# Inverse norms of q and k moved from ScalarE and VectorE to GpSimd, with a k|v projection in two parts, in a two-layer hybrid transformer kernel

## The chip, the cores and the metric

The kernel runs on one core of one Trainium2 chip. The metric is the device time of one execution in microseconds. All numbers are float32; TensorE gets its operands as pairs of a high and a low half (`_hi` and `_lo`), and a product is three matmuls, hi by hi, hi by lo and lo by hi.

## What is computed

Two layers work on 512 image tokens `x` and 256 context tokens `ctx`, 1024 wide. The change touches the part that makes q, k and v for the attention of 4 heads:

```python
q = (rmsnorm(q_lat, qc_g) @ w_q_up).reshape(b, n, MLA_HEADS, QK_DIM)
kv = (rmsnorm(kv_lat, kvc_g) @ w_kv_up).reshape(b, n, MLA_HEADS, NOPE_DIM + V_DIM)
q_nope = rmsnorm(q[..., :NOPE_DIM], qn_g)
q_rope = rmsnorm(q[..., NOPE_DIM:], qr_g)
k_nope = rmsnorm(kv[..., :NOPE_DIM], kn_g)
v = kv[..., NOPE_DIM:]
k_rope = rmsnorm(k_rope, kr_g)
if rope is not None:
    q_rope = apply_axial_rope(q_rope, cos[:, None, :], sin[:, None, :])
    k_rope = apply_axial_rope(k_rope, cos, sin)
```

`rmsnorm(x, g)` is `x * rsqrt(mean(x*x) + 1e-6) * g`. NOPE_DIM and V_DIM are 128, the rope part is 64 wide. Around it stand the adaptive norms, the other inputs of the mixer (pooling, gated convolution), softmax, the output projection and a feed-forward block with a convolution. In the second layer only x goes on, so q is made for 4 tiles of 128 tokens there, and for 6 in the first; k and v are made for 6 in both.

## The kernel before

Each engine has its own program, and the order in it is written out by hand; semaphores with counted values tie them together. PSUM is four slots of two banks (2 x 512 columns), used in turn. A `Job` is one use of a slot: `open` waits until its use before is read out, `filled` and `ready` say that TensorE has written it, `last_read` and `taken` that it is read out.

The stage of this change comes after the latents are projected, normed and transposed. For each tile t of 128 tokens:

- TensorE: `project_q(t)` (L808), `project_kv(t)` (L819: 3 matmuls of 512 columns for k, 3 for v, into the two banks of one slot), then `turn(t-1)` (L830), four transposes of q and four of k, and `turn_rope(t-2)` (L843).
- ScalarE, `stats(t)` (L1240): the square of q (L1248), a copy of q into `qn` (L1252), the square of k into `kn` (L1255), the roots of the mean squares (`root_part`, L1237) for the rope part of q, the plain part of q, and k, with the copy `v_hi` (L1259) before the last. Then `turned_hi(t-1)` (L1270), q and k, and `rope_out(t-2)` (L1278).
- VectorE, `normed(t)` (L1730): the sums over heads (L1720), the reciprocals of the roots (L1727), the scaling of q's rope part (L1744), the scaling of k (L1749, out of PSUM), and `v_lo` (L1753, through L1568), whose end frees the slot. Then `turned_lo(t-1)` (L1569).
- GpSimd: it first turns k_rope for all tiles (`rotate`, L559 to L565), then for each q tile it scales the plain part of q (L624), turns the rope part (L634, L636, L640), and makes its high half (L643) and low half (L645) in `q_rs`.

`b_rot` counts 5 steps a tile: L634, L636, L640, high, low. Between tile 1 and tile 2, k_rope is transposed (`krT`), copied out by ScalarE in two copies (L1327, L1328) and halved by VectorE. After the tiles come the scores: the first part of the first score needs tiles 0 to 3, the second part the k of tiles 4 and 5, that is, tile 5's turned slot read out. The table for Exp is loaded by an activation on `warm` (L1334) before the last `turned_hi`.

## Time and profile before

| | us |
|---|---|
| median of 3 runs | 1451.29 |
| lowest and highest | 1451.26, 1451.75 |
| the profiled execution | 1451.35 |
| its span | 1449.6 |

The profile comes from one execution. Its span is measured from the first to the last instruction, so 1.75 us of the execution's own time lie outside it. Times in a row count from the start of the span. In rows of instructions in order of time, the first number is the start, the second the time taken (of all together where `x2` or more stand there), then engine, line, operation, what it writes and reads with its shape, and in brackets how long the engine stood idle just before and who ended that. PE is TensorE, PEld its weight loads, DVE VectorE, ACT ScalarE, POOL GpSimd.

### The profile page before, as it was taken

The numbers are of one execution on the slowest core, as the hardware profiler recorded it, in microseconds if no ns is written. First come the engines' busy times: TensorE is split into PE (matmuls) and PEld (weight loads), VectorE is DVE, ScalarE is ACT, GpSimd is POOL, SyncE is SP. The second block draws the span as 40 slices with busy tenths as digits, with TensorE's granted clock in tenths as the row PEclk, the third lists the DMA queues.
The fourth block names the chain that finished last, engine by engine and source line by source line (L and its number), as shares of the span: only waits on it lengthen the run. The fifth ranks groups of instructions, "written<-read, shape, count | busy, mean of one in ns | idle before, by whom it ended". The sixth has DMA issues, their size and how long they took to land.

```text
span 1449.6 us, 20646 instructions
## 1 busy us (share of the span) xinstructions
PE 1416.5 (98%) x7940; PEld 1224.0 (84%) x7940; DVE 996.3 (69%) x1532; ACT 521.2 (36%) x841; POOL 86.7 (6%) x125
## 2 busy tenths in 40 slices
PE   6999899999999999999999999989999999999998
PEld 3788798889888888888888888878999888888887
DVE  5587887779866666666575678788667555555555
ACT  4352865243231122122221225476445323223322
POOL 0023700000000000000000000350000000000000
PEclk9999999999999999999999999999999999999999
DMA  9742012423543333324333412301032223322324
GB/s 389 296 131 88 1 45 73 146 88 119 184 146 117 94 122 117 121 81 158 116 100 102 144 45 64 111 15 56 4 103 91 98 90 100 99 87 89 112 91 142
DMA packets 42968, 158.62 MB, mean 109 GB/s; under 512 B 5152, under 2 KB 6560, under 8 KB 41760
## 3 DMA queue, kind: packets, MB, share of 16 engines
q1 hardware_dynamic: 42912, 157.87, 32.7%
q8 instruction: 36, 0.59, 0.2%
q14 instruction: 20, 0.16, 0.0%
HBM read 155.76 MB, written 2.10 MB: 109 GB/s over the span
## 4 chain that ended last, share of the span: by engine, by line
PE 84%; DVE 9%; ACT 3%; DMA 2%; issue 2%; SPq 0%; DVEq 0%; ACTq 0%
PE ps L734 68%; PE ps L653 4%; PE ps L655 4%; PE ps L654 4%; DVE w_lo L1428 1%; DMA ada_step<-in_w_step 1%; DVE tmp L1553 1%; DVE H_lo L1562 1%; PE ps L882 1%; PE ps L667 1%; DVE ss L1495 1%; DVE nmax L1771 1%; DMA w_raw<-in_w_main 1%; DVE pt_lo L1568 1%; ACT w_hi L1072 1%
## 5 line engine op out<-in xcount | busy, mean ns | idle before, releaser
L734 PE MATMUL ps<-H_hi,w_hi 128*128 128x512 f32 (+1 forms) x1280 | 448.8, 351 | 3.9 <-DVE H_lo L1562 2.6
L734 PE MATMUL ps<-H_lo,w_hi 128*128 128x512 f32 (+1 forms) x1280 | 447.4, 350 | 0.0
L734 PE MATMUL ps<-H_hi,w_lo 128*128 128x512 f32 (+1 forms) x1280 | 447.1, 349 | 0.0
L1072 ACT ACTIVATE w_hi<-w_raw 128x1024 fp32r<-128x1024 f32 x180 | 187.5, 1055 | 421.8 <-PE ps L734 368.8
L734 PEld LDWEIGHTS ps<-H_hi,w_hi 128*128 128x128 f32 x1280 | 242.3, 189 | 37.4 <-DVE H_lo L1562 3.8
L734 PEld LDWEIGHTS ps<-H_hi,w_lo 128*128 128x128 f32 x1280 | 242.2, 189 | 31.6
L734 PEld LDWEIGHTS ps<-H_lo,w_hi 128*128 128x128 f32 x1280 | 242.3, 189 | 30.8
L1575 DVE SCALAR_TENSOR_TENSOR X<-ps,mod,X 128x512 f32<-128x512 f32 (+1 forms) x296 | 181.1, 645 | 110.4 <-PE ps L734 88.1
L1428 DVE TENSOR_TENSOR w_lo<-w_raw,w_hi 128x1024 fp32r<-128x1024 f32 x180 | 221.7, 1242 | 37.3 <-ACT w_hi L1072 36.3
L734 PE MATMUL ps<-inner_hi,w_hi 128*128 128x512 f32 (+1 forms) x528 | 188.1, 356 | 0.3 <-DVE X L1575 0.3
L734 PE MATMUL ps<-inner_lo,w_hi 128*128 128x512 f32 (+1 forms) x528 | 187.5, 355 | 0.0
L734 PE MATMUL ps<-inner_hi,w_lo 128*128 128x512 f32 (+1 forms) x528 | 187.0, 354 | 0.0
L1926 DVE SCALAR_TENSOR_TENSOR tmp<-ps,vec,tmp 128x511 f32<-128x511 f32 (+1 forms) x132 | 87.3, 661 | 132.6 <-ACT tmp L1399 124.9
L1439 DVE SCALAR_TENSOR_TENSOR ada_out<-ada_raw,cb 128x1024 f32<-128x1024 f32 x107 | 130.7, 1222 | 5.5 <-DVE mod L1445 0.8
L734 PEld LDWEIGHTS ps<-inner_hi,w_hi 128*128 128x128 f32 x528 | 100.3, 190 | 15.0 <-DVE X L1575 0.5
L734 PEld LDWEIGHTS ps<-inner_lo,w_hi 128*128 128x128 f32 x528 | 100.2, 190 | 13.8
L734 PEld LDWEIGHTS ps<-inner_hi,w_lo 128*128 128x128 f32 x528 | 100.0, 189 | 14.1
L1399 ACT ACTIVATE tmp<-ps,vec 128x768 f32<-128x768 f32 (+1 forms) x44 | 35.0, 795 | 198.5 <-PE ps L734 198.5
L1942 DVE TENSOR_TENSOR ff_v<-tmp,ps 128x768 f32<-128x768 f32 (+1 forms) x44 | 36.1, 820 | 74.7 <-PE ps L734 74.4
L1402 ACT ACTIVATE tmp<-tmp 128x768 f32<-128x768 f32 (+1 forms) x44 | 32.6, 740 | 71.3 <-DVE tmp L1926 71.3
L1125 ACT ACTIVATE H_hi<-tmp,mod 128x256 fp32r<-128x256 f32 (+1 forms) x67 | 38.4, 574 | 39.8 <-DVE tmp L1553 39.8
L1079 ACT ACTIVATE tmp<-X 128x256 f32<-128x256 f32 (+1 forms) x61 | 29.4, 487 | 63.7 <-DVE X L1575 54.9
(210 smaller groups left out, 1836.7 us busy)
## 6 DMA issues: line engine op xcount, KB each, us to landing
w_raw<-in_w_main SPq DMA_DIRECT2D x182, 512.0 KB, 3.3
ada_raw<-in_w_ada SPq DMA_DIRECT2D x73, 512.0 KB, 4.1
ada_step<-in_w_step SPq DMA_DIRECT2D x7, 2048.0 KB, 16.7
X<-in_x SPq DMA_DIRECT2D x2, 1024.0 KB, 6.5
cb<-in_cvec SPq DMA_DIRECT2D x2, 1024.0 KB, 7.2
out_x<-X SPq DMA_DIRECT2D x8, 256.0 KB, 4.0
rtab<-in_rope SPq DMA_DIRECT2D x4, 384.0 KB, 9.2
X<-in_ctx SPq DMA_DIRECT2D x1, 1024.0 KB, 19.5
```

The source lines that it names most:

```text
L653: pe.matmul(out, wh[wsl], xh[xsl], start=first, stop=False)
L654: pe.matmul(out, wh[wsl], xl[xsl], start=False, stop=False)
L655: return pe.matmul(out, wl[wsl], xh[xsl], start=False, stop=last)
L734: ins = pe.matmul(job.ps(a, b), ww[:, wsl], xx[:, xk, a:b], start=first and n == 0, stop=last and n == 2)
L1072: act.activation(w_hi[c % 4][:], w_raw[c % 2][:], ACT.Copy).then_inc(chunk_hi, 1)
L1125: act.activation(H[0][:, kk, a:b], tmp[kk % 2][:, a:b], ACT.Identity, bias=mod[L][:, sg, m:m + 1]).then_inc(h_hi[nn], 1)
L1399: act.activation(tmp[par][:, 0:w], g.ps(0, w), ACT.Copy, scale=tap).then_inc(ff_mid[L], 1)
L1428: dve.tensor_tensor(w_lo[c % 4][:], w_raw[c % 2][:], w_hi[c % 4][:].bitcast(F32), ALU.subtract).then_inc(chunk_lo, 1)
L1439: dve.scalar_tensor_tensor(ada_out[:], ada_raw[n % 2][:], 1.0, cb[n >= ADA_A2][:, s], ALU.mult, ALU.mult, accum_out=mod[L][:, s, bass.ds(c ...
L1575: last = dve.scalar_tensor_tensor(xo, job.ps(a - o, b - o), mod[L][:, s, bass.ds(gate + m, 1)], xo, ALU.mult, ALU.add)
L1926: ins = dve.scalar_tensor_tensor(y, g.ps(a + s0, b - 1 + s0), vec[:, bass.ds(L * V_LAYER + V_FC + FT * tap + t, 1)], y, ALU.mult, ALU.add)
L1942: u.last_read(dve.tensor_tensor(ff_v[:, 0:w], tmp[par][:, 0:w], u.ps(0, w), ALU.mult))
```

## The change

**Power instead of root and reciprocal.** ScalarE's `root_part` and VectorE's `inverse` are gone. VectorE adds EPS times the width to the sums (`with_eps`), and GpSimd raises the result to the power -0.5 (`inverse_root_q`, 8 columns, and `inverse_root_k`, 4 columns), reading a tile of -0.5. The missing square root of the width goes into the gains (`rtab`, `qg`). VectorE waits for `b_rc` of GpSimd before it scales q and k.

**Place of the powers.** Those of tile 0 stand within `rotate`, those of tile t+1 behind the addition that ends the turn of tile t. The high half of the turned q becomes a ScalarE copy, `rotated_hi(t-1)`, in `stats(t)` between the square of k and `v_hi`.

**k|v.** Where the slot is the one of the tile before, the three k matmuls wait only for the scaling of that tile's k (`k_nm`) and raise `k_full` for ScalarE's square; the three v matmuls wait for the slot as before.

**Last tile, table.** For tile 5 k is halved ahead of q; its `v_lo` comes after `turned_lo(4)`. The Exp table is loaded right behind the latents' root.

```diff
@@ GpSimd
-        def rotate(src, n, tab, done, before, scratch):
+        def rotate(src, n, tab, done, before, scratch, root_q, root_k):
             pool.tensor_tensor(a, src, rtab[:, tab, 0:n], ALU.mult).then_inc(done, 1)
+            root_q(0)
             for h in range(2):
...
             last.then_inc(done, 1)
+            root_k(0)
             pool.wait_ge(done, before + 2)
...
+            def inverse_root_q(t):
+                pool.wait_ge(b_rt[L], parts(L, t, "q"))
+                pool.tensor_tensor(part_rms[:, t % 2, 0:8], part_sums[:, t % 2, 0:8], part_pow[:, 0:8], ALU.pow).then_inc(b_rc[L], 1)
+
+            def inverse_root_k(t):
+                pool.wait_ge(b_rt[L], parts(L, t, "k"))
+                pool.tensor_tensor(part_rms[:, t % 2, 8:12], part_sums[:, t % 2, 8:12], part_pow[:, 8:12], ALU.pow).then_inc(b_rc[L], 1)
...
                 pool.tensor_tensor(src, rgain[:], rope_b[:], ALU.add).then_inc(b_rot[L], 1)
-                pool.wait_ge(b_rot[L], 5 * t + 3)
+                if t + 1 < qtok(L):
+                    inverse_root_q(t + 1)
+                if t + 1 < TOK:
+                    inverse_root_k(t + 1)
+                pool.wait_ge(b_rot[L], 5 * t + 4)
                 hi, lo = (q_rs[L][t % 2][:, :, ROPE * n:ROPE * (n + 1)] for n in range(2))
-                pool.tensor_copy(hi.bitcast(F32R), src).then_inc(b_rot[L], 1)
-                pool.wait_ge(b_rot[L], 5 * t + 4)
                 pool.tensor_tensor(lo, src, hi, ALU.subtract).then_inc(b_rot[L], 1)
@@ TensorE, project_kv
-                job.open(pe)
+                follows = t and JOB[("kv", t), L] - JOB[("kv", t - 1), L] == 4
+                if follows:
+                    pe.wait_ge(k_nm[L], t)
+                else:
+                    job.open(pe)
+                mm3(job.ps(0, 512), kvl, (slice(None), tsl), slot(c0 + C_HD + 2), (slice(None), slice(0, 512)),
+                    True, True).then_inc(k_full[L], 1)
+                if follows:
+                    job.open(pe)
@@ ScalarE
             act.activation(lat_ss[:], lat_ss[:], ACT.Sqrt).then_inc(lat_rt[L], 1)
+            act.activation(warm[:, 0:1], ones[:, 0:1], ACT.Exp)
...
+            def rotated_hi(t):
+
+                act.wait_ge(b_rot[L], 5 * t + 3)
+                src = qn[t % 2][:, 0:ROPES].rearrange("p (h f) -> p h f", h=HEADS)
+                act.activation(q_rs[L][t % 2][:, :, 0:ROPE].bitcast(F32R), src, ACT.Copy).then_inc(b_rot[L], 1)
...
+                act.wait_ge(k_full[L], t + 1)
+                act.activation(kn[t % 2][:], job.ps(0, 512), ACT.Square).then_inc(b_sq[L], 1)
+                if 0 < t <= qtok(L):
+                    rotated_hi(t - 1)
                 job.ready(act)
...
-                root_part(t, "k")
@@ VectorE
+            def with_eps(t, first, last):
+
+                cols = slice(4 * KINDS.index(first), 4 * KINDS.index(last) + 4)
+                dve.wait_ge(b_sum[L], sections(L, t, last))
+                dve.tensor_tensor(part_sums[:, t % 2, cols], part_sums[:, t % 2, cols], part_eps[:, cols],
+                                  ALU.add).then_inc(b_rt[L], 1)
...
                 if t < qtok(L):
-                    inverse(t, "rope", "nope")
+                    dve.wait_ge(b_rc[L], parts(L, t, "q"))
...
+                if t < TOK - 1:
+                    value_lo(t)
...
+            value_lo(TOK - 1)
             turned_lo(TOK - 1)
```

GpSimd in layer 0, from k_rope's turn into tile 1, before:

```order
29 L559 TENSOR_TENSOR win_p<-latr,rtab 128x384
30 L561 TENSOR_TENSOR win_r<-latr,rtab 128x6x32 x2
31 L565 TENSOR_TENSOR latr<-win_p,win_r 128x6x64
32 L624 TENSOR_TENSOR qn_128<-qn_128,part_rms 128x512
33 L634 TENSOR_TENSOR rgain<-qn_128,rtab 128x256
34 L636 TENSOR_TENSOR rope_b<-qn_128,rtab 128x4x32 x2
35 L640 TENSOR_TENSOR qn_128<-rgain,rope_b 128x256
36 L643 CAST q_rs_124<-qn_128 128x4x64
37 L645 TENSOR_TENSOR q_rs_124<-qn_128,q_rs_124 128x4x64
38 L624 TENSOR_TENSOR qn_129<-qn_129,part_rms 128x512
```

The same place in the changed kernel:

```order
32 L566 TENSOR_TENSOR win_p<-latr,rtab 128x384
33 L630 TENSOR_TENSOR part_rms<-part_sums,part_pow 128x8
34 L569 TENSOR_TENSOR win_r<-latr,rtab 128x6x32 x2
35 L634 TENSOR_TENSOR part_rms<-part_sums,part_pow 128x4
36 L574 TENSOR_TENSOR latr<-win_p,win_r 128x6x64
37 L642 TENSOR_TENSOR qn_130<-qn_130,part_rms 128x512
38 L652 TENSOR_TENSOR rgain<-qn_130,rtab 128x256
39 L654 TENSOR_TENSOR rope_b<-qn_130,rtab 128x4x32 x2
40 L658 TENSOR_TENSOR qn_130<-rgain,rope_b 128x256
41 L630 TENSOR_TENSOR part_rms<-part_sums,part_pow 128x8
42 L634 TENSOR_TENSOR part_rms<-part_sums,part_pow 128x4
43 L665 TENSOR_TENSOR q_rs_126<-qn_130,q_rs_126 128x4x64
```

The powers of tile 0 (rows 33 and 35) stand inside k_rope's turn, those of tile 1 (41 and 42) behind the addition that ends tile 0's turn (L658, once L640), and the cast is gone.

ScalarE in layer 0, tile 2 and what follows it, before:

```order
103 L1248 ACTIVATE q_sq_122<-ps 128x768
104 L1252 ACTIVATE qn_128<-ps 128x768
105 L1255 ACTIVATE kn_130<-ps 128x512
106 L1237 ACTIVATE part_rms<-part_sums,vec 128x4 x2
107 L1259 ACTIVATE v_hi<-ps 128x4x128
108 L1237 ACTIVATE part_rms<-part_sums,vec 128x4
109 L1270 ACTIVATE q_hi<-ps,qg 128x4x128
```

In the changed kernel:

```order
102 L1273 ACTIVATE q_sq_124<-ps 128x768
103 L1277 ACTIVATE qn_130<-ps 128x768
104 L1280 ACTIVATE kn_132<-ps 128x512
105 L1263 ACTIVATE q_rs_127<-qn_131 128x4x64
106 L1284 ACTIVATE v_hi<-ps 128x4x128
107 L1298 ACTIVATE q_hi<-ps,qg 128x4x128
```

Three roots are gone, and the copy of tile 1's turned q (row 105) stands between the square of tile 2's k and the copy of its v; in tile 1 the copy of tile 0's q stands in the same place.

## Rows read from the trace of the kernel before

**Rows 1.** The page, busy us, share of the span and instructions, TensorE and others.
```profile
PE 1416.5 (98%) x7940; PEld 1224.0 (84%) x7940; DVE 996.3 (69%) x1532; ACT 521.2 (36%) x841; POOL 86.7 (6%) x125
```

**Rows 2.** Busy time of each engine by stretch, the two stretches of the head projections.
```profile
core 0: us, PE busy (x) PEld busy (x) DVE busy (x) ACT busy (x) POOL busy (x), PEclk, DMA share, GB/s
...
140.00:182.00 42.00, 38.28 (x222) 30.94 (x222) 35.66 (x75) 35.45 (x74) 30.85 (x47) 1.00 0.00 1
...
950.00:984.00 34.00, 29.23 (x160) 23.02 (x160) 28.70 (x56) 26.21 (x53) 18.39 (x29) 0.95 0.00 1
```

**Rows 3.** Waits of TensorE's weight loads, 138 to 182: total, times, longest.
```profile
PEld ps L653 <- DVE v_lo L1568: 2.7, 4, 1.0
PEld ps L837 <- issue: 2.4, 2, 2.1
```

**Rows 4.** The same, 952 to 988.
```profile
PEld ps L653 <- DVE v_lo L1568: 2.2, 2, 1.3
```

**Rows 5.** In order of time, GpSimd, layer 0, k_rope's turn and tile 0.
```profile
142.48 1.16 POOL L561 TENSOR_TENSOR win_r<-latr,rtab 128x192 f32<-128x192 f32 x2
...
143.72 1.16 POOL L565 TENSOR_TENSOR latr<-win_p,win_r 128x384 f32<-128x384 f32 x1
...
144.84 1.03 POOL L624 TENSOR_TENSOR qn<-qn,part_rms 128x512 f32<-128x512 f32 x1
...
147.48 0.80 POOL L640 TENSOR_TENSOR qn<-rgain,rope_b 128x256 f32<-128x256 f32 x1
```

**Rows 6.** In order of time, ScalarE, tile 1 and the square of tile 2's q.
```profile
145.56 0.60 ACT L1255 ACTIVATE kn<-ps 128x512 f32<-128x512 f32 x1
...
147.23 0.79 ACT L1327 ACTIVATE kr_hi<-ps 64x768 fp32r<-64x768 f32 x1
...
150.03 0.81 ACT L1248 ACTIVATE q_sq<-ps 128x768 f32<-128x768 f32 x1
```

**Rows 7.** In order of time, VectorE, scaling in tile 1 and 4, first sums.
```profile
147.07 0.62 DVE L1744 TENSOR_TENSOR qn<-qn,part_rms 128x256 f32<-128x256 f32 x1
...
147.81 0.69 DVE L1749 TENSOR_TENSOR kn<-ps,part_rms 128x512 f32<-128x512 f32 x1
...
151.20 1.00 DVE L1720 TENSOR_REDUCE part_sums<-q_sq 128x4 f32<-128x256 f32 x2
...
156.03 1.00 DVE L1720 TENSOR_REDUCE part_sums<-q_sq 128x4 f32<-128x256 f32 x2
...
163.13 0.88 DVE L1744 TENSOR_TENSOR qn<-qn,part_rms 128x256 f32<-128x256 f32 x1
...
166.66 1.00 DVE L1720 TENSOR_REDUCE part_sums<-q_sq 128x4 f32<-128x256 f32 x2
```

**Rows 8.** Instructions of one line: count, duration in ns least/median/most, first and last start.
```profile
L1237 ACT ACTIVATE part_rms<-part_sums,vec x32: 283/297/325, 142.6 to 972.9; 128x4 f32<-128x4 f32 x32
...
L1727 DVE RECIPROCAL part_rms<-part_rms x22: 164/178/196, 143.3 to 973.3; 128x4 f32<-128x4 f32 x12, 128x8 f32<-128x8 f32 x10
...
L607 POOL TENSOR_TENSOR win_r<-win_r,vec x12: 199/202/1181, 96.4 to 935.4; 128x8 f32<-128x8 f32 x12
...
L1445 DVE TENSOR_TENSOR mod<-mod,vec x8: 155/160/208, 138.1 to 852.3; 128x7 f32<-128x7 f32 x2, 128x5 f32<-128x5 f32 x2, 128x8 f32<-128x8 f32 x2, 128x16 f32<-128x16 f32 x1
```

**Rows 9.** In order of time, the end of the stage in layer 0, TensorE and ScalarE.
```profile
170.34 0.63 PE L837 MATMUL ps<-ident,qn 128*128 128x128 f32 x4 [1.88 <-POOL qn L624]
...
170.49 1.28 ACT L1334 ACT_TABLE_LOAD   x1
...
174.06 0.39 PE L653 MATMUL ps<-k_hi,q_hi 128*128 128x256 f32 x1 [0.66 <-DVE k_lo L1569]
```

**Rows 10.** In order of time, layer 1, GpSimd's turn of tile 0 and tile 1's scaling.
```profile
953.63 0.74 POOL L640 TENSOR_TENSOR qn<-rgain,rope_b 128x256 f32<-128x256 f32 x1
...
953.97 0.68 DVE L1744 TENSOR_TENSOR qn<-qn,part_rms 128x256 f32<-128x256 f32 x1
```

**Rows 11.** Busy time by stretch, with the granted clock, near the end in layer 1.
```profile
974.00:976.00 2.00, 1.67 (x6) 1.54 (x7) 1.44 (x3) 1.97 (x4) 0.00 (x0) 0.57 0.01 4
```

More of the change, by code:

```diff
@@ L359, in halves @@
         nq = qtok(L)
+        if t == TOK - 1 and t < nq:
+            return 2 * t + {"k": 1, "q": 2}[kind]
         return 2 * t + {"q": 1, "k": 2}[kind] if t < nq else nq + t + 1
@@ L548, in _ @@
         pool.memset(lat_ss[:], 1.0).then_inc(consts, 1)
+        pool.memset(part_eps[:, 0:4], ROPE * EPS)
+        pool.memset(part_eps[:, 4:12], NOPE * EPS)
+        pool.memset(part_pow[:], -0.5)
         pool.memset(part_sums[:], 1.0).then_inc(consts, 1)
@@ L640, in _ @@
                 pool.tensor_tensor(src, rgain[:], rope_b[:], ALU.add).then_inc(b_rot[L], 1)
-                pool.wait_ge(b_rot[L], 5 * t + 3)
+                if t + 1 < qtok(L):
[3 more added lines that the diff above has]
+                pool.wait_ge(b_rot[L], 5 * t + 4)
                 hi, lo = (q_rs[L][t % 2][:, :, ROPE * n:ROPE * (n + 1)] for n in range(2))
-                pool.tensor_copy(hi.bitcast(F32R), src).then_inc(b_rot[L], 1)
-                pool.wait_ge(b_rot[L], 5 * t + 4)
                 pool.tensor_tensor(lo, src, hi, ALU.subtract).then_inc(b_rot[L], 1)
+            for t in range(qtok(L) + 1, TOK):
+                inverse_root_k(t)
     @block.tensor
@@ L822, in project_kv @@
                 job = Job(JOB[("kv", t), L])
-                job.open(pe)
-                for half in range(2):
-                    cols = slice(512 * half, 512 * (half + 1))
-                    last = mm3(job.ps(512 * half, 512 * (half + 1)), kvl, (slice(None), tsl), slot(c0 + C_HD + 2),
-                               (slice(None), cols), True, True)
-                job.filled(last)
+                follows = t and JOB[("kv", t), L] - JOB[("kv", t - 1), L] == 4
[7 more added lines that the diff above has]
+                    job.open(pe)
+                job.filled(mm3(job.ps(512, 1024), kvl, (slice(None), tsl), slot(c0 + C_HD + 2), (slice(None), slice(512, 1024)),
+                               True, True))
             def turn(t):
@@ L1267, in turned_hi @@
                 job.ready(act)
-                for kind, dst, o, scale in (("q", q, 0, qg[:, 0:1]), ("k", k, 512, V(L, V_KN))):
+                for kind, dst, o, scale in turned_parts(t):
                     if kind == "k" or t < qtok(L):
@@ L1333, in _ @@
                 rope_out(t - 2)
-            act.activation(warm[:, 0:1], ones[:, 0:1], ACT.Exp)
             turned_hi(TOK - 1)
+            if qtok(L) == TOK:
+                rotated_hi(TOK - 1)
             for t in range(TOK - 2, TOK):
@@ L1721, in sums @@
                                   ALU.add).then_inc(b_sum[L], 1)
-            def inverse(t, first, last):
-                x = part_rms[:, t % 2, 4 * KINDS.index(first):4 * KINDS.index(last) + 4]
-                dve.wait_ge(b_rt[L], sections(L, t, last))
-                dve.reciprocal(x, x).then_inc(b_rc[L], 1)
-                dve.wait_ge(b_rc[L], parts(L, t, "k" if last == "k" else "q"))
+            def with_eps(t, first, last):
[3 more added lines that the diff above has]
+                                  ALU.add).then_inc(b_rt[L], 1)
             def normed(t):
@@ L1736, in normed @@
                     sums(t, "nope", q_sq[L][:, ROPES:HEADS * HQ], NOPE)
+                    with_eps(t, "rope", "nope")
                 dve.wait_ge(b_sq[L], parts(L, t, "k"))
                 sums(t, "k", kn[m][:], NOPE)
+                with_eps(t, "k", "k")
                 if t < qtok(L):
-                    inverse(t, "rope", "nope")
+                    dve.wait_ge(b_rc[L], parts(L, t, "q"))
                     Job(JOB[("q", t), L]).taken(dve)
@@ L1753, in normed, with turned_parts @@
                 job.last_read(lo_half(v[1][:, :, tsl], job.ps(512, 1024).rearrange("p (h f) -> p h f", h=HEADS), v[0][:, :, tsl]))
+            def turned_parts(t):
+                order = (("q", q, 0, qg[:, 0:1]), ("k", k, 512, qg[:, 1:2]))
+                return order[::-1] if t == TOK - 1 else order
             def turned_lo(t):
@@ L1758, in turned_lo @@
                 job = Job(JOB[("turn", t), L])
-                for kind, dst, o, scale in (("q", q, 0, qg[:, 0:1]), ("k", k, 512, V(L, V_KN))):
+                for kind, dst, o, scale in turned_parts(t):
                     if kind == "k" or t < qtok(L):
```

31 lines of the change are left out of this document (14 added, 17 removed).

## The prediction

> **What bounds the kernel now.** The first thing to read is the busy share of the page: TensorE is busy 98% of the span [rows 1]. Whatever lengthens or shortens the waits of TensorE therefore moves the end almost one for one, and anything on another engine counts only through such a wait. The table of stretches then shows where there is anything to win or lose: the stretch of the head projections, 140 to 182 us in layer 0 and 950 to 984 us in layer 1, is the one in which the others are nearly as full as TensorE: in layer 0 VectorE 35.7, ScalarE 35.5 and GpSimd 30.9 of 42 us, and in it TensorE has holes [rows 2]. The waits of TensorE's weight loads in that stretch name the holes: 2.7 us in 4 waits for v_lo, which frees the accumulator of the k|v projection, and 2.4 us, nearly all of it one wait, for the last tile's normed q [rows 3]; in layer 1 the v_lo wait in front of a projection is 2.2 us in two waits [rows 4]. So at most some 5 us a layer are there to be won, and the change aims at about half of them.
>
> All four engines run the tiles in a fixed order, one tile of 128 tokens about every 5 us. GpSimd is the one that is late at the start: its turning of k_rope (L559, L561, L565) ends at 144.84, and only then comes q of tile 0; it leaves the rotation of tile 0 (L640, from 147.48, 0.80 long) at 148.28 [rows 5]. At that time VectorE has long scaled q and k of tile 1, at 147.07 and 147.81 [rows 7], and ScalarE is already copying k_rope out, from 147.23 [rows 6]. In the kernel before nobody but the rope transposes and the next copy of q waits for this lateness.
>
> **Roots off ScalarE, power on GpSimd.** ScalarE loses 32 roots of 0.297 us and VectorE 22 reciprocals of 0.178 us; VectorE gains 22 additions of EPS, of the form of L1445, 0.160 us, each of which has to wait for the reduction before it (0.03 us past its end), so VectorE's work for a tile stays at 4.8 to 4.9 us against 4.83 now (151.20 to 156.03) [rows 7, 8]. GpSimd gains 22 powers. No row shows a power. The nearest is a multiplication of the same shape, 128x8: 199 ns at the least, 202 in the median, and 1181 where it lies beside a long VectorE addition [rows 8]. I take 0.30 us for 8 columns and 0.25 for 4, near the low end since the shape is the same and only the arithmetic is dearer, and keep 0 and 1.18 us as ends.
>
> The Trainium skill (GPSIMD Engine Reference, 3.1 Elementwise) says that branching on data costs about 12 cycles an element at 1.2 GHz; an estimate by it for 8 elements a lane is 0.08 us on top of the row's 0.20, so 0.28 us, and the sum would be 0.1 us a layer lower. No run here shows it yet.
>
> **Where the powers stand is what costs.** The order of GpSimd's instructions puts the powers of tile t+1 behind the rotation of tile t. Step by step for layer 0: the power of q of tile 0 waits for the sums and the added EPS on VectorE, and starts near 142.8, where the next piece of the k_rope turn used to start at 142.48: 0.3 us. It takes 0.3, the power of k 0.25. So the k_rope turn ends 0.8 us later, near 145.65, and the rotation of tile 0, which is 3.4 us behind that [rows 5], at 149.05. Only then can the power of tile 1 run. VectorE gets it at 149.4 instead of having its own reciprocal by 147.07: q of tile 1 is scaled 2.3 us late, k of tile 1 (149.75 against 147.81) 1.9 us late [rows 7]. TensorE's k half of tile 2 now waits for exactly that k, so its earlier start by one v_lo (0.6 us) is spent there.
>
> **The copy that moved to ScalarE.** The high half of the turned q (a GpSimd cast) is now a ScalarE copy of about 0.36 us, placed between the square of k and the copy of v of the next tile. ScalarE runs in order: in tile 1 it ends the square of k at 146.05 (145.56 and 0.49 to the next) and then stands until GpSimd has turned tile 0, at 149.1. Queued behind it are v of tile 1, both copies of k_rope, q and k of tile 0 and the square of q of tile 2. Before, 1.67 us lay between the square of k and the k_rope copy (147.23 less 145.56) [rows 6]; now 0.49, a wait of 3.1, 0.36 and 0.48, so 4.4: the k_rope copy and all behind it come 2.7 us later, the square of q of tile 2 near 152.75 instead of 150.03. VectorE's first sum of tile 2 comes at 153.85 instead of 151.20 [rows 7], 2.65 us late, and the transposes of tile 1 wait on TensorE for k_rope's bank.
>
> **What is won back.** From tile 2 on GpSimd needs 4.15 us and two powers, 4.7, a tile, VectorE 4.88, ScalarE less. Before, VectorE's starts of tiles 2 and 5 are 15.46 us apart (151.20 to 166.66), 5.15 a tile: it waited for TensorE's k|v in each, and one scaling of q was stretched to 0.88 us [rows 7]. Three tiles at 4.88 are 14.64, so 0.8 us comes back; if the stretch, 0.45 us, returns, 0.35. This is the gain of the k half with its own waits: real, and about a third of the loss. Layer 0 at tile 5: 1.85 to 2.3 us late.
>
> **The tail.** The table load of Exp (1.28 us) stands before the last q and k copies; TensorE's last turn starts at 170.34 and its k transposes would release them near 171.4, so removing the load is worth 0.5 us, not 1.28 [rows 9]. It moves behind the root of the latents, 50 us ahead of the stage, where ScalarE has idle time and TensorE does not wait: nothing. The k copies ahead of q gain nothing by themselves, since the second part of the first score waits until both are done and the bank is released by the last. Against this the last scaling of q on GpSimd now stands behind the power of k and the low half of tile 4, which used to be through before: 0.7 us. So the tail is 0.15 to 0.3 us longer. v's rest moved behind the split of the tile before costs nothing in layer 0; in layer 1 its bank is the one that the first score needs, which now starts up to 0.7 us later.
>
> **The sum.** I carried these durations through both orders, row by row; for the kernel before this gives tile 5's k within 0.6 us of the trace. Layer 0 comes out 2.8 us later at the first row maximum; with the stretch of 0.45 us counted as gone, and the load's place in doubt, I take 2.5. Layer 1 has the same order and the same place: its rotation of tile 0 runs from 953.63 to 954.37 while tile 1's q is scaled at 953.97 [rows 10]; it has only four q tiles, so two k-only tiles are left in which k waits for the power. It comes out 3.0 later. There the clock falls too: TensorE is granted 0.57 of full speed on average in 974 to 976 [rows 11], so part of it is at 1.2 GHz, after three waits of TensorE; with longer waits there the low stretch may grow by the 0.3 us I add. Sum 2.5 and 3.3 = 5.8 us. The profiled execution took 1451.35 us with a span of 1449.6; the median is 1451.29, the same within 0.06. Forecast 1457.1 us. A difference under 0.2% (2.9 us) can't be told from none here.
>
> **The rivals.** (a) *The late start is made up for*: TensorE's holes close so far that the tiles run at its own 4.8 us, and the fall of the clock in layer 1 is gone. For it: the v_lo waits are real, 2.7 and 2.2 us [rows 3, 4]. Against it: GpSimd sets the start, and 0.35 us a tile is all there is. It gives 1452.8: 2.65 late, less 4 tiles by 0.35 and 0.5 of table in each layer, is 0.75 each. Chance 0.17. (b) *Faster*: the powers cost nothing, and the waits of VectorE and ScalarE on GpSimd in tile 1 are absorbed before TensorE needs k and q of tile 2. Then the gain is what v_lo costs now, up to 0.6 us in six places, and the table: 1451.3 less 4 is 1447.3. It decides if the rotation of tile 0 ends before about 147.0, where tile 1's scaling stood; it ends at 148.28 already now [rows 5]. Chance 0.08. (c) *A dear power*: at 0.8 and 0.5 us GpSimd's tile is 5.45 us and it becomes the bound of every tile: 5.1 and 4.7 late, 1461.1; at 1.18 and 0.8 some 17 us, 1468. The point is 0.7 us for both powers, where GpSimd passes VectorE's 4.88. For it: the 1181 ns; against: that figure comes beside one VectorE addition. Chance 0.13. (d) The forecast, 0.62, with its own range of 1454.3 to 1459.5 (powers free and the stretch gone, 1.2 and 1.8 late; powers of 0.5 and 0.4, 3.8 and 3.8, with clock).
>
> GpSimd and VectorE share their path into SBUF, says the Trainium skill (GPSIMD Engine Reference, 1. Specifications), for VectorE instructions with two SBUF inputs; the rows that were stretched, 882 against 426 ns, are of that kind. By it the added EPS and the powers could stretch each other by tenths of a microsecond, which lies within the range.
>
> **How the numbers follow.** Low end 1452.5: (b) and the part of (a) below it are left out, about 0.12. High end 1462.5: the dearer half of (c) is left out, 0.07. Slower by over 0.2%: (d) and (c), 0.75; within 0.2%: (a), 0.17; faster: (b), 0.08.
>
> **What would show it.** The GpSimd power row near 0.3 us; ScalarE waiting about 3 us for GpSimd's rotation in front of the q_rs copy of tile 1, in each layer, and about 1 us at later tiles; VectorE waiting 1.5 us and more for the power before the scaling of tile 1's q, and nearly nothing later; first sum of tile 2 at 153.5 to 154; tiles 2 to 5 at 4.9 us apart; v_lo gone from TensorE's waits in front of projections, k (kn) and k_rope's bank there instead; first row maximum 2.5 us later in layer 0 than at 175.55. I am wrong if ScalarE's wait in tile 1 is under 1 us, if a power is over 0.7 us, or if the later tiles run under 4.7 us apart.

## The result and the profile after

The changed kernel takes 1476.68 us (median; 1474.76 to 1477.10), the kernel before on the same chip 1451.51 (1451.26 to 1451.75). The ratio is 1.0171 with a 95% interval of 1.0159 to 1.0184: 25 us slower. The forecast was 1457.1 with a range up to 1462.5, so the sign was right and the size was not.

The page, busy time of each engine, after (against [rows 1]):

```profile
PE 1423.0 (97%) x7940; PEld 1228.7 (83%) x7940; DVE 995.2 (68%) x1534; ACT 519.3 (35%) x819; POOL 108.7 (7%) x140
```

GpSimd has 22 us more work, from 86.7 to 108.7, and the kernel became 25 us longer. An engine that is busy for 7% of the span does not look like a bound; in the stretch of the head projections it is one. By stretch, with the columns of [rows 2], after (the stage is 13 us longer in layer 0 now, so the window is wider):

```profile
138.00:192.00 54.00, 42.29 (x217) 34.00 (x217) 36.24 (x71) 30.85 (x55) 43.49 (x53) 0.91 0.00 1
178.00:180.00 2.00, 0.00 (x0) 0.00 (x0) 0.69 (x3) 2.00 (x4) 2.00 (x2) 1.00 0.00 0
180.00:182.00 2.00, 0.00 (x0) 0.00 (x0) 1.76 (x3) 0.06 (x1) 2.00 (x4) 0.92 0.00 0
182.00:184.00 2.00, 1.96 (x10) 1.99 (x11) 0.84 (x2) 0.00 (x0) 1.92 (x4) 0.50 0.00 0
```

GpSimd, 43.5 of 54 us, is now the fullest engine, ahead of TensorE. From 178 to 182 us TensorE does nothing at all, and right behind it its granted clock is 0.50, 1.2 GHz. It falls to 0.50 in 148 to 150 and 162 to 164 us too, each time behind four microseconds in which TensorE was busy for 1.45 and 2.21 us. Before, layer 0 had 1.00 over the whole stretch [rows 2].

One line's instructions on GpSimd, after, the two powers: count, duration in ns least/median/most.

```profile
L630 POOL TENSOR_TENSOR part_rms<-part_sums,part_pow x10: 1647/1650/1662, 141.8 to 984.4; 128x8 f32<-128x8 f32 x10
...
L634 POOL TENSOR_TENSOR part_rms<-part_sums,part_pow x12: 1007/1012/1015, 144.7 to 995.5; 128x4 f32<-128x4 f32 x12
```

These two rows are the main finding. The prediction had 0.30 and 0.25 us. The multiplication of the same shape, 202 ns [rows 8], was no guide, and 1.18 us, which the prediction kept as the upper end, was too low as well. The spread over ten is 15 ns: this is a price, not a disturbance.

In order of time, after, GpSimd from the end of tile 0's rotation to tile 1's scaling, and the scalings of the next tiles (against [rows 5]):

```profile
149.28 0.73 POOL L658 TENSOR_TENSOR qn<-rgain,rope_b 128x256 f32<-128x256 f32 x1
149.96 1.65 POOL L630 TENSOR_TENSOR part_rms<-part_sums,part_pow 128x8 f32<-128x8 f32 x1
151.58 1.01 POOL L634 TENSOR_TENSOR part_rms<-part_sums,part_pow 128x4 f32<-128x4 f32 x1
152.56 0.73 POOL L665 TENSOR_TENSOR q_rs<-qn,q_rs 128x256 f32<-128x256 f32 x1
153.24 1.04 POOL L642 TENSOR_TENSOR qn<-qn,part_rms 128x512 f32<-128x512 f32 x1
...
160.56 1.04 POOL L642 TENSOR_TENSOR qn<-qn,part_rms 128x512 f32<-128x512 f32 x1
...
167.33 1.04 POOL L642 TENSOR_TENSOR qn<-qn,part_rms 128x512 f32<-128x512 f32 x1
```

From 160 to 170 us no row of GpSimd has a wait ahead of it: it runs from one instruction into the next, and its tile is 6.77 us (160.56 to 167.33). The prediction's 4.15 us without powers and 1.65 + 1.01 make 6.81. Before it was 5.15 a tile, and VectorE's and TensorE's work set it.

The same seen from VectorE, in order of time, after (against [rows 7]):

```profile
151.65 0.43 DVE L1776 TENSOR_TENSOR qn<-qn,part_rms 128x256 f32<-128x256 f32 x1 [2.43 <-POOL part_rms L630]
...
156.01 0.99 DVE L1750 TENSOR_REDUCE part_sums<-q_sq 128x4 f32<-128x256 f32 x2
...
162.47 1.00 DVE L1750 TENSOR_REDUCE part_sums<-q_sq 128x4 f32<-128x256 f32 x2
...
169.22 1.00 DVE L1750 TENSOR_REDUCE part_sums<-q_sq 128x4 f32<-128x256 f32 x2
```

And as a list of waits, 138 to 192 us, after (total, times, longest; against [rows 3]):

```profile
ACT q_rs L1263 <- POOL qn L658: 10.4, 5, 4.9
DVE qn L1776 <- POOL part_rms L630: 7.2, 6, 2.4
PEld ps L675 <- DVE kn L1780: 5.7, 4, 2.2
PEld ps L864 <- issue: 5.3, 3, 4.6
```

The largest waits of ScalarE and VectorE behind the stage's first square end at GpSimd. TensorE's waits for k (kn) in front of the k half are those that the own waits of the halves were to shorten; in layer 0 v_lo is no longer the one that is waited for there, k is.

A yardstick for the rest is **the length of the stage**: from ScalarE's first square of q to VectorE's first row maximum. It leaves out how early or late the stage begins. In layer 0 it was 34.84 us (140.71 to 175.55) and is 48.06 (139.65 to 187.71); in layer 1 it was 30.95 and is 41.84. Together 24.1 us, which is the whole loss within about 1 us; nothing outside the stage needs an explanation. Layer 0's 13.2 us split into 5.9 up to the first sum of tile 2, 4.5 in the three tiles from there to tile 5, and 2.8 in the tail.

### The profile page after: what moved, and what is told of

Same layout as the page of the kernel before. It is cut to its first block, busy times and chain, and to the rows that moved or that the text cites. A ratio compares the mean times of both kernels' runs of the same rounds, so it can differ in the third digit from the quotient of the medians.

```text
span 1472.9 us, 20629 instructions
## 1 busy us (share of the span) xinstructions
PE 1423.0 (97%) x7940; PEld 1228.7 (83%) x7940; DVE 995.2 (68%) x1534; ACT 519.3 (35%) x819; POOL 108.7 (7%) x140
## 4 chain that ended last, share of the span: by engine, by line
PE 83%; DVE 8%; POOL 3%; ACT 2%; DMA 2%; issue 2%; SPq 0%; POOLq 0%; DVEq 0%; ACTq 0%
PE ps L756 68%; PE ps L675 4%; PE ps L676 3%; PE ps L677 3%; DVE w_lo L1457 1%; POOL part_rms L630 1%; DMA ada_step<-in_w_step 1%; PE ps L909 1%; DVE ss L1524 1%; POOL part_rms L634 1%; PE ps L689 1%; DMA w_raw<-in_w_main 1%; DVE nmax L1812 1%; DVE tmp L1582 1%; DVE pt_lo L1597 1%
```

## The experiments

The theory: the mechanism of rival (c), *a dear power*, with the powers in GpSimd's own queue in each tile, costs some 18 us, and what the forecast described (late rotation, ScalarE's wait for it) costs the rest. The rival theory: the order and its waits cost nearly all of it. The expectations call a "hand-worked sequence" what the prediction used too: the durations of the rows carried through each engine's order, row by row, here with the measured price of the power. Each ratio is taken against the kernel before run beside it, whose median lay between 1450.5 and 1451.5 us.

### The price taken away

```diff
-  pool.tensor_tensor(part_rms[:, t % 2, 0:8], part_sums[:, t % 2, 0:8], part_pow[:, 0:8], ALU.pow).then_inc(b_rc[L], 1)
+  pool.tensor_tensor(part_rms[:, t % 2, 0:8], part_sums[:, t % 2, 0:8], part_pow[:, 0:8], ALU.mult).then_inc(b_rc[L], 1)
```

The same is done for the 4 columns of k.

> The changed kernel with a multiplication in place of each of the 22 powers, on the same engine, tiles and waits. It leaves out the inverse norms of q's and k's parts (their sums are multiplied by -0.5 instead), so the rest is computed at another scale. Theory, the price: the power measures 1.65 us for 128x8 and 1.01 us for 128x4 where the prediction had 0.30 and 0.25, and this alone makes GpSimd the bound of every tile (tiles 6.8 us apart). Working the sequence of one tile through with 0.2 us for each, the shift of the first row maximum against the kernel before falls from 12.9 to 2.5 us in layer 0 and from 10.8 to 2.7 in layer 1, so 1451.5 + 5.2 = 1456.7 us, tiles 4.8 to 5.0 us apart. Rival, the place: the powers stand in GpSimd's order behind the rotation and in front of q's scaling, and the halves and the moved copy add their own waits; most of the 25 us is then left, 1470 us or more, whatever the operation costs.

Measured: 1457.71 us, ratio 1.0048 (1.0033 to 1.0064), some 7 us over the kernel before. The stage is 2.7 us longer in layer 0 and 3.7 in layer 1. The operation alone is worth 18 us (1.0171 less 1.0048, of 1451; by the medians 19); the place and the waits are worth the 7 that remain. This run is the experiment of the forecast: a power of 0.20 us where it had assumed 0.30 and 0.25, and 1457.7 us where it had forecast 1457.1. Against the kernel before run beside it (1450.5) that is 7.0 us, where 5.8 was forecast. In order of time, this kernel, ScalarE and VectorE in tile 1, then VectorE's first sums:

```profile
148.24 0.42 ACT L1263 ACTIVATE q_rs<-qn 128x256 fp32r<-128x256 f32 x1 [2.76 <-POOL qn L658]
...
148.41 0.43 DVE L1776 TENSOR_TENSOR qn<-qn,part_rms 128x256 f32<-128x256 f32 x1 [0.99 <-POOL part_rms L630]
148.75 0.68 DVE L1780 TENSOR_TENSOR kn<-ps,part_rms 128x512 f32<-128x512 f32 x1
...
152.89 0.99 DVE L1750 TENSOR_REDUCE part_sums<-q_sq 128x4 f32<-128x256 f32 x2
...
157.84 1.00 DVE L1750 TENSOR_REDUCE part_sums<-q_sq 128x4 f32<-128x256 f32 x2
...
163.07 1.01 DVE L1750 TENSOR_REDUCE part_sums<-q_sq 128x4 f32<-128x256 f32 x2
...
168.31 1.01 DVE L1750 TENSOR_REDUCE part_sums<-q_sq 128x4 f32<-128x256 f32 x2
```

The stage begins 0.68 us earlier here (140.03) than in the kernel before. ScalarE waits 2.8 us for the rotation, and the first sum of tile 2 is 2.4 us late. But the next tiles are 4.95, 5.23 and 5.24 us apart, not 4.88. From 157.84 to 168.31 VectorE has no wait on record:

```profile
157.84:168.31 10.47, 10.00 (x60) 8.23 (x60) 10.15 (x21) 8.50 (x16) 8.93 (x17) 1.00 0.01 2
```

VectorE, 10.15 of 10.47 us, is full (third of the busy times, as in [rows 2]). In order of time, the same kernel, the EPS additions of tile 2 and tile 3, then one pass between VectorE and GpSimd:

```profile
153.92 0.17 DVE L1757 TENSOR_TENSOR part_sums<-part_sums,part_eps 128x8 f32<-128x8 f32 x1
...
158.88 0.45 DVE L1757 TENSOR_TENSOR part_sums<-part_sums,part_eps 128x8 f32<-128x8 f32 x1
...
159.95 0.16 DVE L1757 TENSOR_TENSOR part_sums<-part_sums,part_eps 128x4 f32<-128x4 f32 x1
160.19 0.33 POOL L634 TENSOR_TENSOR part_rms<-part_sums,part_pow 128x4 f32<-128x4 f32 x1 [0.59 <-DVE part_sums L1757]
...
163.81 0.73 POOL L658 TENSOR_TENSOR qn<-rgain,rope_b 128x256 f32<-128x256 f32 x1
...
164.12 0.45 DVE L1757 TENSOR_TENSOR part_sums<-part_sums,part_eps 128x8 f32<-128x8 f32 x1
...
165.19 0.17 DVE L1757 TENSOR_TENSOR part_sums<-part_sums,part_eps 128x4 f32<-128x4 f32 x1
```

VectorE's addition of EPS to the 8 sums of q takes 0.17 us in tile 2, where GpSimd does nothing beside it, and 0.45 in the later tiles, where it lies beside GpSimd's last step of the rotation (L658) and ends with it. That is the difference between 4.95 and 5.24 us. It repeats: the addition for k (159.95) lets GpSimd's instruction for k go, GpSimd works through scaling and rotation without a wait until 164.5, the stretched addition ends there, and the next addition for k comes at 165.19, 5.24 us after the one before. From tile 2 on VectorE's scaling of k also starts just as GpSimd's instruction for k ends, a wait too short to be listed. ScalarE's copy is not in this loop: the square of q that is queued behind it ends near 162.5, and VectorE takes it up at 163.07, straight behind its work for the tile before. This is read from the rows; no run takes the stretch away alone. The expectation of the run with the copy back on GpSimd, below, still puts the loop through ScalarE's wait.

### How the time answers to the price

The same with one of the two powers left in, and with q's power run a second time for each tile but the first (`part_two` is read by nobody):

```diff
                     inverse_root_q(t + 1)
+                    pool.tensor_tensor(part_two[:], part_sums[:, t % 2, 0:8], part_pow[:, 0:8], ALU.pow)
```

> The changed kernel with the multiplication in place of q's power (128x8) alone; k's power (128x4, 1.01 us) stays. It leaves out the inverse norms of q's parts. Theory: beyond what is hidden, each added us of GpSimd's work comes out in every tile. By the hand-worked sequence 12.6 us over the kernel before where it has 5.2 for two multiplications and 23.6 for two powers: 1451.3 + 12.6 = 1463.9 us, a little over that since the measured times of the others were 0.9 to 1.8 above it. Rival, a step: once the powers together pass some length an order of waits tips over and nearly the whole loss is there; then this run is at 1472 or more, or, if the length isn't reached, at 1458.

> The changed kernel with the multiplication in place of k's power (128x4) alone; q's power (128x8, 1.65 us) stays. It leaves out the inverse norms of k's parts. By the hand-worked sequence 15.0 us over the kernel before: 1451.3 + 15.0 = 1466.3 us or a little more. Rival: k's power, which stands behind q's and ahead of the low half and of q's scaling, is the one that stalls the tile; then this run is near that with multiplications alone, 1458 us.

> The changed kernel with q's power of each tile but the first run a second time, into a tile that nobody reads: five more powers of 1.65 us on GpSimd in each layer, a tile where q's are computed (three in layer 1). If GpSimd's own sequence sets the tiles, as the 6.8 us between tiles say, each comes out in full: 1.65 us x 8 = 13.2 us over the changed kernel, 1476.7 + 13 = 1490 us. Rival: the tile is set by waits for VectorE or ScalarE, and GpSimd has slack; then the added powers are hidden in part, under 1485 us.

| kernel | power of q and k of a tile, us | median, us | ratio (95%) | stage longer, layer 0 and 1 |
|---|---|---|---|---|
| multiplications | 0.20 and 0.26 | 1457.71 | 1.0048 (1.0033 to 1.0064) | 2.7, 3.7 |
| k's power alone | 0.21 and 1.08 | 1465.66 | 1.0100 (1.0083 to 1.0116) | 7.6, 7.1 |
| q's power alone | 1.65 and 0.20 | 1468.18 | 1.0118 (1.0101 to 1.0135) | 9.1, 7.4 |
| the changed kernel | 1.65 and 1.01 | 1476.68 | 1.0171 (1.0159 to 1.0184) | 13.2, 10.9 |
| q's power twice | 3.29 and 1.01 | 1488.88 | 1.0258 (1.0241 to 1.0275) | 21.9, 15.9 |

Expected were 1456.7, 1463.9 "or a little over", 1466.3 "or a little more", and 1490: all four within about 2 us. The three runs with a multiplication in them leave out the inverse norms that it stands for. There is no step. Between the changed kernel and the doubled power 12.2 us come for 8 added instructions of 1.65 us, 13.2: nearly every one in full. Between the multiplications and the changed kernel 10 x 1.45 and 12 x 0.75 us are added, 23.5 us, and 18 to 19 arrive: the first tenths of each tile go into GpSimd's slack. The doubled power's tiles, in order of time, VectorE:

```profile
167.58 1.01 DVE L1752 TENSOR_REDUCE part_sums<-q_sq 128x4 f32<-128x256 f32 x2
...
175.92 1.00 DVE L1752 TENSOR_REDUCE part_sums<-q_sq 128x4 f32<-128x256 f32 x2
...
184.27 1.00 DVE L1752 TENSOR_REDUCE part_sums<-q_sq 128x4 f32<-128x256 f32 x2
```

8.34 us apart, where the changed kernel has 6.77: 1.57 more for one more power.

### The price by itself

```diff
+        for n, x in enumerate((2.0, -0.5)):
+            pool.memset(probe[n][:], x).then_inc(b_ms[0], 1)
+        for m, (op, other) in enumerate(((ALU.pow, 1), (ALU.pow, 0), (ALU.mult, 1))):
+            for n in (1, 2, 4, 8, 16, 32):
...
+                pool.tensor_tensor(probe[2][:, 0:n], probe[0][:, 0:n], probe[other][:, 0:n], op).then_inc(b_ms[0], 1)
```

> The kernel before with 18 added instructions at the start of GpSimd's program, one behind the other, on tiles that nothing else uses: the power of 128 x 1, 2, 4, 8, 16 and 32 values 2.0 to the exponent -0.5, the same with exponent 2.0, and the multiplication of the same tiles. Only their rows count, not the time. Theory: the power is paid by the element, about 0.16 us a column on a start of 0.37 us (1.65 us for 8 columns and 1.01 for 4 in the changed kernel give this line), so 0.53 us for 1 column, 0.69 for 2, 2.9 for 16, 5.5 for 32, the same for both exponents; the multiplication stays near 0.20 us. Rival: most of the cost is a fixed start that comes with every power, or it depends on the exponent; then 16 and 32 columns stay well under those numbers, or the two exponents differ.

Groups of instructions by shape, GpSimd (xcount, then busy us and mean ns of one). The first two rows are from the stretch of the powers to -0.5, the third is a power to 2.0, the last two are from the stretch of the multiplications:

```profile
L559 POOL TENSOR_TENSOR probe<-probe,probe 128x32 f32<-128x32 f32 x1 | 5.4, 5427 | 0.1
...
L559 POOL TENSOR_TENSOR probe<-probe,probe 128x1 f32<-128x1 f32 x1 | 0.6, 561 | 0.1
...
L559 POOL TENSOR_TENSOR probe<-probe 128x32 f32<-128x32 f32 x1 | 5.4, 5445 | 0.1
...
L559 POOL TENSOR_TENSOR probe<-probe,probe 128x32 f32<-128x32 f32 x1 | 0.3, 312 | 0.1
...
L559 POOL TENSOR_TENSOR probe<-probe,probe 128x8 f32<-128x8 f32 x1 | 0.2, 207 | 0.1
```

For the exponent -0.5 the six widths took 561, 711, 1007, 1637, 2900 and 5427 ns: 157 ns a column of 128 (4866 ns over 31 columns) on 0.40 us. The exponent 2.0 costs the same (561 to 5445). The line was drawn beforehand from 8 and 4 columns alone and gave 0.53, 0.69, 2.9 and 5.5. The multiplications took 191 to 608 ns with no order in their width (312 for 32 columns, 608 for 2), so a price a column can't be read from them; the three from 542 to 608 ran beside two long VectorE instructions (L1560 and L1569 of that kernel). With 312 ns for 32 columns it is far under the power's 5427. The power's cost is paid by the column, and by this line joining q's and k's powers in one instruction would save no more than the 0.40 us (an estimate; it was not run).

### The copy alone, and the copy undone

```diff
@@ ScalarE, kernel before with the copy moved (undone the other way round)
                     root_part(t, "nope")
+                if 0 < t <= qtok(L):
+                    rotated_hi(t - 1)
                 act.activation(v[0] ...
@@ GpSimd
-                pool.tensor_copy(hi.bitcast(F32R), src).then_inc(b_rot[L], 1)
```

> The kernel before with one edit: the copy of the rotated q's high half moves from GpSimd to ScalarE, at the place where the change has it (behind the square root's step of the next tile, ahead of v's eviction); square root and reciprocal stay. By the hand-worked sequence ScalarE waits about 3 us for GpSimd's rotation in the second tile, and the first row maximum comes 3.3 us later in layer 0 and 2.8 in layer 1: 1451.5 + 6.1 = 1457.6 us. Rival: the copy is free, since ScalarE has slack and GpSimd gains 0.5 us a tile: 1451.5 or under.

> The changed kernel with one part undone: the copy of the rotated q's high half is back on GpSimd. That takes ScalarE's waits for the rotation away (10.4 us in five tiles of layer 0) and puts 0.47 us a tile on GpSimd. If GpSimd is the bound of every tile, the waits on ScalarE cost nothing and the copy costs its own time: by the hand-worked sequence 1476.7 + 2.8 = 1479.5 us. Rival: the order on ScalarE is what costs; then the time falls by several us, to 1472 or less.

> The changed kernel with the multiplication in place of each power and the copy of the rotated q's high half back on GpSimd; the inverse norms of q's and k's parts are left out, as in the run with the multiplication. That run left 7 us, with tiles 5.24 us apart, in a loop that passes through ScalarE's wait for the rotation. Theory: with the power cheap, the copy on ScalarE is what costs the rest, as the run with that copy alone says (6.5 us), so nearly all of it goes: 1451.5 us or a little over. Rival, by the hand-worked sequence: the powers behind the rotation still hold q's scaling back in the second tile, 1451.5 + 4.5 = 1456 us, and the copy only takes the place of that wait.

The copy alone, put on the kernel before: 1457.24 us, ratio 1.0044 (1.0029 to 1.0060). Expected 1457.6. One cast of 0.4 us that moves to an engine with slack costs 6.4 us. ScalarE in tile 1 of this kernel, in order of time:

```profile
148.95 0.42 ACT L1242 ACTIVATE q_rs<-qn 128x256 fp32r<-128x256 f32 x1 [1.66 <-POOL qn L640]
```

ScalarE stands 1.7 us in front of it, with v, k_rope and the next tile's squares queued behind; the first sum of tile 2 is 2.0 us late, and the tiles are 5.5 us apart. Why 5.5 shows in GpSimd's low half and VectorE's scaling of q's rope part, in order of time:

```profile
161.18 0.74 POOL L643 TENSOR_TENSOR q_rs<-qn,q_rs 128x256 f32<-128x256 f32 x1 [1.19 <-ACT q_rs L1242]
161.29 0.90 DVE L1752 TENSOR_TENSOR qn<-qn,part_rms 128x256 f32<-128x256 f32 x1
```

The low half now waits for ScalarE's copy and so comes to lie beside the scaling, which takes 0.90 to 0.91 us in each of the tiles 2 to 5, where it took 0.43, 0.49, 0.88 and 0.43 before. TensorE's k|v still waits for the v_lo that follows it (0.5 us), ScalarE's square of k for TensorE (0.55), and VectorE's sum of k for that square (0.2).

With the powers in place, the copy back on GpSimd doesn't help: 1478.74 us, ratio 1.0192 (1.0175 to 1.0209), 2 us over the changed kernel by the medians. The intervals overlap, but the stages are 2.5 us longer than the changed kernel's (expected 2.8) and the tiles 7.08 us. The 10.4 us of ScalarE's waits are there because GpSimd is late, and taking them away gains nothing while GpSimd is the bound; most of its own 0.47 us a tile then comes out.

With multiplications, the theory said that the copy's return would win back nearly all of the 7 us, and **it was wrong**: 1456.77 us, ratio 1.0034 (1.0022 to 1.0047), still about 5 us over the kernel before, with the stage 2.7 and 2.1 us longer. Its rival, the hand-worked sequence, had 1456. That fits the rows above: ScalarE's wait was not what set the later tiles. GpSimd's scalings of this kernel, in order of time:

```profile
155.65 1.05 POOL L642 TENSOR_TENSOR qn<-qn,part_rms 128x512 f32<-128x512 f32 x1
...
160.70 1.05 POOL L642 TENSOR_TENSOR qn<-qn,part_rms 128x512 f32<-128x512 f32 x1
...
165.74 1.05 POOL L642 TENSOR_TENSOR qn<-qn,part_rms 128x512 f32<-128x512 f32 x1
```

Tiles of 5.05 us, and GpSimd without a wait in them: 4.15 and the cast 0.47 and two multiplications fill the tile. The first sum of tile 2 is 1.6 us late through the powers' place alone, 2.0 through the copy alone, 2.4 through both. The two don't add up; in each of the three runs the first wait is for the same thing, the rotation of tile 0.

### The parts that were to win something

> The kernel before with one edit: the k half of the k|v projection waits only for the previous tile's k and reports by itself, and k's squares wait for it alone; v's half waits for v's low half as before. By the hand-worked sequence 0.5 us is won in layer 0 and 0.25 in layer 1: 1451.5 - 0.75 = 1450.8 us. Rival: TensorE only waits elsewhere, for the same v ahead of the upper half: 1451.5.

```diff
@@ kernel before; TensorE, with k_full raised behind the k half
-                job.open(pe)
+                if follows:
+                    pe.wait_ge(k_nm[L], t)
...
@@ ScalarE
-                job.ready(act)
+                act.wait_ge(k_full[L], t + 1)
                 act.activation(kn[t % 2][:], job.ps(0, 512), ACT.Square).then_inc(b_sq[L], 1)
```

1450.84 us, ratio 1.0001 (0.9992 to 1.0010): no difference that can be told. The stage itself is 0.8 us shorter in layer 0 (0.5 was expected) and 0.1 longer in layer 1 (0.25 shorter was expected). If the 0.7 in all is real, it is below what the times resolve.

> The same with one more edit: the load of the exponential's table stands behind the copy of the second-last tile's rotation, where ScalarE waits for GpSimd, and not ahead of that copy. The load takes 1.28 us and lies ahead of the last q and k rows' copies in the kernel before. By the hand-worked sequence 1.5 us is won in both layers together: 1451.5 - 1.5 = 1450.0 us. Rival: those copies wait for TensorE's transposes anyway and the load is hidden already: the same as the halves alone, 1450.8.

```diff
-            act.activation(warm[:, 0:1], ones[:, 0:1], ACT.Exp)
             turned_hi(TOK - 1)
-            for t in range(TOK - 2, TOK):
-                rope_out(t)
+            rope_out(TOK - 2)
+            act.activation(warm[:, 0:1], ones[:, 0:1], ACT.Exp)
+            rope_out(TOK - 1)
```

1450.12 us, ratio 0.9997 (0.9988 to 1.0007), the stage 0.9 us shorter and 0.2 longer, the same as with the halves alone: the rival was right. ScalarE, in order of time:

```profile
171.73 0.69 ACT L1276 ACTIVATE q_hi<-ps,qg 128x512 fp32r<-128x512 f32 x1 [1.35 <-PE ps L845]
...
173.50 1.28 ACT L1342 ACT_TABLE_LOAD   x1
```

Where the table load was, ScalarE now waits 1.35 us for TensorE's transposes. The load cost next to nothing where it stood [rows 9]. This was the version meant to beat both kernels; it does not measurably.

> The changed kernel with one part undone: both halves of the k|v projection wait together again, and k's squares wait for both. With GpSimd as the bound of every tile the halves can neither win nor lose: by the hand-worked sequence 0.0 us against the changed kernel, 1476.5 us. Rival: TensorE's earlier start on k's half does win the half microsecond in each layer that the prediction gave it; then this run is 0.5 to 1 us slower.

> The changed kernel with two parts undone: the last tile's low half of v is written at its old place in VectorE's order, ahead of q's and k's low halves, and the last tile's q is split ahead of k. By the hand-worked sequence 0.0 to -0.2 us against the changed kernel: 1476.5 us. Rival: both gained what they were made for at the stage's end, some 0.7 us a layer; then this run is 1 to 1.5 us slower.

```diff
@@ changed kernel, the first
-                if follows:
-                    pe.wait_ge(k_nm[L], t)
-                else:
-                    job.open(pe)
+                job.open(pe)
@@ changed kernel, the second (q and k; v)
-                return order[::-1] if t == TOK - 1 else order
+                return order
...
-                if t < TOK - 1:
-                    value_lo(t)
+                value_lo(t)
```

Halves undone: 1476.17 us, ratio 1.0176 (1.0158 to 1.0193). v and k undone: 1475.09, ratio 1.0164 (1.0147 to 1.0181). Both lie within the interval of the changed kernel (1.0159 to 1.0184), as expected; in the stage's length they differ from it by 0.1 us or less over both layers (24.0 and 24.1). Beside a bound on GpSimd these parts neither win nor lose in sum. In layer 0 one can see what k first is worth: TensorE's loads of the first score, in order of time, in the changed kernel and then with v and k undone.

```profile
186.20 0.19 PEld L675 LDWEIGHTS ps<-k_hi,q_hi 128*128 128x128 f32 x1 [0.46 <-DVE q_lo L1598]
```

```profile
187.59 0.19 PEld L675 LDWEIGHTS ps<-k_hi,q_hi 128*128 128x128 f32 x1 [1.20 <-DVE k_lo L1598]
```

Its stage starts 0.84 us later (140.49), so the first score comes 0.55 us earlier with k first; layer 1 gives the same amount back. There the first score takes the slot of tile 5's k|v, and v_lo, which frees it, now comes behind the split of tile 4. Layer 1, the changed kernel, in order of time:

```profile
997.86 0.68 DVE L1597 TENSOR_TENSOR v_lo<-ps,v_hi 128x512 fp32r<-128x512 f32 x1
...
998.72 0.29 PEld L675 LDWEIGHTS ps<-k_hi,q_hi 128*128 128x128 f32 x1 [0.63 <-issue]
```

TensorE stands 0.63 us until v_lo has ended; with v and k undone it doesn't wait there. The prediction had named this as up to 0.7 us.

## Why the prediction was wrong, and where it was right

**The price of a power: the failed step.** The prediction said: "I take 0.30 us for 8 columns and 0.25 for 4, near the low end since the shape is the same and only the arithmetic is dearer, and keep 0 and 1.18 us as ends." Measured: 1.65 and 1.01. With 0.20 us in its place the same kernel takes 1457.7 us, with the measured price 1476.7: the term was short by about 18 us and everything else together by 1 to 2. Two errors lie in that one sentence. The shape of a small instruction does not carry its price; 128x8 costs 0.2 us as a multiplication and 1.65 as a power. And 1.18 us was no upper end: it is the longest of 12 multiplications that lay beside VectorE's work [rows 8], a row on contention, which says nothing on arithmetic. No row of the kernel before could have capped a power, and the range should have been open above, with rival (c) far over 0.13.

The estimate that stood beside it, from the Trainium skill (GPSIMD Engine Reference, 3.1 Elementwise), took 10 ns a column for branching on data and gave 0.28 us. The measured 157 ns a column disagree by a factor of 16, and the measurement decides: what that section states for branching is no price for a power, for which it gives none.

**Rival (c) was the case.** Its mechanism (GpSimd the bound of every tile from about 0.7 us for both powers on) is what the profile shows: tiles of 6.77 us against VectorE's 4.88. Its curve of times was good too: it had 17 us for powers of 1.18 and 0.8, and carried on to 1.65 and 1.01 the same sequence gives 23.6 (12.9 and 10.8), where the stages show 24.1 (13.2 and 10.9).

**Where the powers stand: right.** Seen in the run with multiplications, all against the kernel before and from the stage's start: rotation of tile 0 at 148.9 (forecast 149.05), q of tile 1 scaled 2.0 us late (2.3), k 1.6 (1.9).

**The copy on ScalarE: right.** Its wait in tile 1 was 2.8 us (3.1), the first sum of tile 2 2.4 us late (2.65). With the dear power the wait is 4.9 us.

**What is won back: wrong, hidden by the larger error.** Tiles at 4.88 us and 0.35 to 0.8 back were forecast; with multiplications tiles 2 to 5 take 15.42 us against 15.46 before. The forecast had the right engine, VectorE, and its work too small: the EPS addition, costed at 0.16 us, takes 0.45 beside GpSimd's rotation, so its tile is 5.24 us and not 4.88. The prediction had named such a stretch of the added EPS and left it within its range; the powers themselves were not what stretched it. That layer 0 came out at 2.7 us where 2.5 was forecast is in part luck: the start was 0.3 us less late than forecast, which made up for most of the gain that did not come.

**The tail.** Forecast 0.15 to 0.3 longer, with 0.5 of it won by the table load. With multiplications it is 0.4 longer (9.28 against 8.89 us from tile 5's first sum to the first row maximum). The load's 0.5 is not there: moved into a pause, it won nothing. In the changed kernel the tail is 2.8 us longer. There TensorE waits 4.6 us for the last scaling of q, and then turns q and k at half its clock. TensorE's last turn, weight loads, in order of time, after (against [rows 9]):

```profile
182.01 0.71 PEld L864 LDWEIGHTS ps<-ident,qn 128*128 128x128 f32 x4 [4.59 <-issue]
182.71 0.87 PEld L867 LDWEIGHTS ps<-ident,kn 128*128 128x128 f32 x4
```

The second row took 0.47 us at full clock. The prediction had thought of the clock in layer 1 alone [rows 11].

**The rest of the sum.** v's rest makes the first score of layer 1 wait 0.63 us, as forecast (up to 0.7), and k first wins 0.55 in layer 0, where nothing was forecast; the halves can't be seen in the changed kernel. The table load behind the latents' root was costed at nothing; the stage's lengths leave no more than 1 us for everything outside the stage, so that stands. Layer 1 with multiplications came 3.7 us late (forecast 3.3), layer 0 2.7 (2.5). Of the 3.3, 0.3 was for the clock in layer 1: it was 0.57 in two stretches of 2 us before (974 to 978), and with multiplications it is 0.50 in three (980 to 986) and 0.83 in the next. The low stretch grew as forecast; its share of the 3.7 was not separated.

**Of the three conditions for being wrong, one came true**: "if a power is over 0.7 us".

## What to carry to other kernels

Before an operation moves to another engine, measure that operation there, in the width that it will have; one row of another operation of the same shape bounds nothing, and where nothing in the trace bounds it, the range has to stay open above. Then add it to that engine's work for one tile and compare with the tile's length: up to the slack it is nearly free, beyond it every instruction comes out in every tile, however small the engine's share of the span (7% here). And an engine with slack is not a free place for an instruction that waits: a copy of 0.4 us on ScalarE cost 6.4 us. It stands in order ahead of work that others need, and what waits for it on GpSimd comes to lie beside a scaling on VectorE that is stretched by it. So add up an engine's work for a tile with the durations that its instructions have beside the other engine's, not with their shortest.

## What was not expected of the hardware

- A power on GpSimd takes 0.40 us and 0.157 us for each column of 128 float32 values (0.56 us for 1, 5.43 for 32), the same for the exponents -0.5 and 2.0. A multiplication of 128x8 takes 0.20.
- In the changed kernel it is steady: 1647 to 1662 ns over ten. It is not so beside any work of VectorE: with k's power alone, the 128x4 power took 1.14 us in six of twelve tiles, those in which VectorE's scaling of q had begun 0.16 us ahead of it, and 1.01 to 1.02 in the others.
- A power does not hold VectorE up, where a rotation step of GpSimd does. In the changed kernel VectorE's scaling of q's rope part, begun during the power of k (at 165.72 us within 165.66 to 166.67), takes 0.43 us, its shortest, and the EPS addition of k during the power of q 0.16. The EPS addition of q takes 0.17 us with GpSimd idle and 0.40 to 0.47 beside the rotation steps L652, L654 and L658.
- A stretch in which TensorE does nothing, 178 to 182 us, is followed by a granted clock of 0.50 in the next two, in a layer that had kept full clock in the kernel before. Standing still alone doesn't do it each time: in layer 1 TensorE stands 3.0 us, to 988.87, and the clock stays at 1.00. With multiplications the stretch of layer 0 has 1.00.
